# Wide products that nobody reads, put between the router's steps on TensorE

## The reference, cut to what matters

```
def ec_moe(h, w_router, w_gate, w_up, w_down):
    xt = h.reshape(n, D)
    aff = jax.nn.softmax((xt @ w_router).astype(jnp.float32), axis=-1)
    cap = CAPACITY_FACTOR * n // N_EXPERTS
    gate, idx = lax.top_k(aff.T, cap)
    xe = jnp.take(xt, idx, axis=0)
    hid = jax.nn.silu(jnp.einsum('ecd,edf->ecf', xe, w_gate)) * jnp.einsum('ecd,edf->ecf', xe, w_up)
    ye = jnp.einsum('ecf,efd->ecd', hid, w_down) * gate[..., None].astype(h.dtype)
    out = jnp.zeros_like(xt).at[idx.reshape(-1)].add(ye.reshape(-1, D))
```

## Time and profile before

| what | value |
|---|---|
| time, median of 3 runs | 1823.35 us |
| the profiled execution's own time | 1822.89 us |
| its span, first to last instruction | 1821.1 us |
| TensorE (PE) busy | 1668.2 us, 92% of the span |
| VectorE, ScalarE busy | 510.3 us, 298.2 us |
| moved by DMA | 638.52 MB, mean 351 GB/s |
| mean granted TensorE clock | 0.984 of full speed |

### The profile page before, as it was taken

The page is one execution under the profiler, slowest core; times in us unless marked ns, Lnnn a source line. Parts: engine busy times, 40 slices in busy tenths (PEclk is TensorE's granted clock), DMA queues, the critical chain, the costliest instruction groups (busy, mean ns, idle before and its releaser), DMA issues.

```text
span 1821.1 us, 19170 instructions
## 1 busy us (share of the span) xinstructions
PE 1668.2 (92%) x7900; PEld 792.5 (44%) x7900; DVE 510.3 (28%) x982; ACT 298.2 (16%) x635; POOL 47.8 (3%) x72
## 2 busy tenths in 40 slices
PE   6999999999999999888898888889888998889897
PEld 3767777778884333332232232323222233223232
DVE  4575647775670201111010111101011111101103
ACT  2453354563330000000000000000000000000001
POOL 2010000011000000000000000000000000000001
PEclk9999999999979999999999999999999999999999
DMA  9873232226587999999999999999999999999996
GB/s 346 285 281 105 71 128 92 93 93 215 221 362 317 425 395 432 427 434 429 431 429 431 429 432 431 428 431 431 430 432 429 432 430 430 431 428 431 431 430 269
DMA packets 65023, 638.52 MB, mean 351 GB/s; under 512 B 5653, under 2 KB 5837, under 8 KB 36557
## 3 DMA queue, kind: packets, MB, share of 16 engines
q1 hardware_dynamic: 61648, 629.83, 83.0%
q0 software_dynamic: 3328, 8.04, 1.4%
HBM read 634.14 MB, written 3.70 MB: 350 GB/s over the span
## 4 chain that ended last, share of the span: by engine, by line
DMA 50%; PE 47%; DVE 3%; issue 0%; ACT 0%; SPq 0%; ACTq 0%; DVEq 0%
DMA ring<-in_w_exp_gate 23%; DMA ring<-in_w_exp_up 23%; PE banks L877 17%; PE banks L1296 15%; DMA ring<-in_w_exp_down 4%; PE banks L1415 2%; PE banks L875 2%; PE banks L829 1%; PE banks L1278 1%; PE banks L892 1%; PE banks L1078 1%; PE banks L1233 1%; PE banks L873 1%; PE banks L1035 1%; PE banks L1009 1%; DMA ring<-in_w_mod 1%
## 5 line engine op out<-in xcount | busy, mean ns | idle before, releaser
L1296 PE MATMUL banks<-ring,O 128*64 128x512 f32 x3048 | 657.0, 582 | 81.7 <-DMA ring<-in_w_exp_up 60.5
L1296 PEld LDWEIGHTS banks<-ring,O 128*64 128x64 f32 x3048 | 211.9, 135 | 528.0 <-issue 421.9
L1415 PE MATMUL banks<-ring,O 128*64 128x512 f32 x1400 | 317.7, 609 | 37.7 <-DMA ring<-in_w_exp_down 33.2
L1415 PEld LDWEIGHTS banks<-ring,O 128*64 128x64 f32 x1400 | 98.9, 140 | 245.4 <-issue 183.8
L877 PE MATMUL banks<-slot_parts,X_parts 128*128 128x512 f32 x672 | 184.3, 403 | 0.0
L2240 DVE TENSOR_TENSOR O<-O,banks 128x512 f32<-128x512 f32 (+1 forms) x48 | 30.9, 644 | 515.7 <-PE banks L1296 487.3
L1724 ACT ACTIVATE O<-banks 128x512 f32<-128x512 f32 (+1 forms) x48 | 23.7, 563 | 736.3 <-PE banks L1296 736.3
L877 PEld LDWEIGHTS banks<-slot_parts,X_parts 128*128 128x128 f32 x672 | 121.2, 188 | 39.4 <-issue 11.8
L2220 DVE TENSOR_TENSOR X<-X,banks 128x512 f32<-128x512 f32 x90 | 61.9, 688 | 190.6 <-PE banks L1278 190.6
L1850 DVE TENSOR_TENSOR slot_parts<-ring,slot_parts 128x512 fp32r<-128x512 f32 x168 | 105.7, 688 | 16.6 <-ACT slot_parts L1471 15.9
L2253 DVE TENSOR_TENSOR O<-banks,O 128x512 f32<-128x512 f32 x32 | 20.7, 686 | 319.4 <-PE banks L1415 319.4
(11 more groups left out here) (296 smaller groups left out, 1136.2 us busy)
## 6 DMA issues: line engine op xcount, KB each, us to landing
ring<-in_w_exp_up SPq DMA_DIRECT2D x61, 2816.0 KB, 33.8
ring<-in_w_exp_gate SPq DMA_DIRECT2D x58, 2816.0 KB, 32.1
ring<-in_w_exp_down SPq DMA_DIRECT2D x29, 3072.0 KB, 28.3
ring<-in_w_exp_down SPq DMA_DIRECT2D x14, 4096.0 KB, 31.6
ring<-in_w_in SPq DMA_DIRECT2D x16, 2048.0 KB, 8.8
ring<-in_w_exp_down SPq DMA_DIRECT2D x24, 1024.0 KB, 33.2
ring<-in_w_mod SPq DMA_DIRECT2D x16, 512.0 KB, 11.4
O<-in_w_mod SPq DMA_DIRECT2D x8, 1024.0 KB, 5.2
```

Source lines behind the costliest of these rows:

```text
L1296: x = pe.matmul(banks[64 * w:64 * w + 64, 3 * m + b, 0:(i1 - i0) * P], xeT[:, 2 * (k % 4) + k // 4, :], w4[:, w, i0 * P:i1 * P], start=(k ...
L1415: x = pe.matmul(banks[64 * w:64 * w + 64, (4 if last else 6) + dc, :], hidT[:, i, 64 * w:64 * w + 64], rows[:, w, dc * BANK:(dc + 1) * BAN ...
```

## The change

35 products are added to TensorE's list, in 12 places (one of them in a loop that runs four times) between the end of the mixer and the first expert's products. Each multiplies 64 columns of the identity with 512 columns of `ring` (the start of quarter 5, the first expert's second up quarter) into partitions 0 to 63 of bank 7 or bank 0. Nobody reads what they write. A wait for that quarter's transfer (`land_u[1]`) is added ahead of them, and a second `wait_job_copied(pe, J_WO[-1])` before the first of them that writes bank 0. Nothing is removed, and the order of all other instructions is as it was.

```diff
+            def keep_clock(n, bank=0):
+                for i in range(n):
+                    pe.matmul(banks[0:64, bank, :], ident[:, 0:64], reg(5 * QUARTER, BANK), start=True, stop=True)
+            pe.wait_ge(land_u[1], 16)
             pe.wait_ge(h2_norm, 1)
             turn_tile(h2, 0)
+            keep_clock(2, 7)
             shift_logits()
+            keep_clock(1, 7)
             pe.wait_ge(h2_norm, 2)
             turn_tile(h2, 1)
+            keep_clock(2, 7)
             pe.wait_ge(shift_row, 1)
             for n in range(2):
                 for b in range(2):
                     logits(n, b)
+                    keep_clock(2, 7)
+            wait_job_copied(pe, J_WO[-1])
             pe.wait_ge(h2_half_done, 1)
             turn_half(h2, 2, 0)
+            keep_clock(1)
             turn_probs(0)
             turn_probs(1)
+            keep_clock(1)
             pe.wait_ge(h2_half_done, 2)
             turn_half(h2, 2, 1)
-            for b in range(2):
-                logits(2, b)
+            keep_clock(2)
+            logits(2, 0)
+            keep_clock(2)
+            logits(2, 1)
+            keep_clock(8)
             wait_job_copied(pe, J_WO[-1])
...
             turn_probs(2)
             pe.wait_ge(rt_part, 1)
             pe.matmul(banks[:, 1, 0:CAP_L], one_expert(0), slots[:, 0:CAP_L], start=True, stop=True).then_inc(rt_first, 1)
+            keep_clock(2)
...
             pe.wait_ge(sel_ready, 2)
             first_gather((2, 3, 6, 7), (1, 2))
+            keep_clock(4)
             pe.wait_ge(rt_part, 2)
             pe.matmul(banks[:, 1, CAP_L:SLOT], one_expert(0), slots[:, CAP_L:SLOT], start=True, stop=True).then_inc(rt_first, 1)
             first_gather((4, 5), (1, 2))
             pe.wait_ge(sel_ready, 3)
             first_gather((2, 3, 6, 7), (0,)).then_inc(xet_done, 1)
             first_gather((0, 1), (1, 2))
+            keep_clock(2)
```

## The result

The changed kernel takes 1849.34 us, the median of 4 runs (1848.85 to 1850.16), against 1823.51 us before: ratio 1.0142, 95% interval 1.0127 to 1.0157, so 25.8 us slower. The forecast was 1846.6 us, in a range of 1841 to 1860.

What follows compares the result with a forecast made beforehand. The path to the first expert products bounds the kernel: 20.84 us of old work plus 31.5 of new replace 29.09, 23.3 later; 1822.89 + 23.3 = 1846.2, median 0.46 higher, forecast 1846.6 us, range 1841 to 1860.

Steps and rivals of the forecast that it cites:

- What bounds the kernel: Way to the first expert products: one microsecond there is one of the whole; the experts behind have no slack.
- The price of one product: Added products, mixer's end to first experts: 0.90 us each at full clock, 35 cost 31.5 us.
- The other work at full clock: TensorE's old router work: turns 2.91, shift 0.50, logits 6.60, probability turns 0.45, two further products 0.63 us together.
- rival B: The clock doesn't hold in the router: 1867 us, or 1880 if it never returns before the experts; chance 0.18.
- The gathers: 40 records before the first expert product: 0.244 us each at either clock, so 9.75 us stay.
- The clock at the first expert products: Clock falls after about 6 us of late narrow gather work; the same 2 us are lost as before the change.
- A: Forecast case: clock holds, products 0.9 us each, 1846.6; own range 1842 to 1851, chance 0.77; low: prices -0.9, clock held -2.0.
- The waits: Router: first tile's logits 531.9, selection start 541.1, slots 549.9 us; 5.6 of the eight products' 7.2 us hold up selection.
- Rival C: Not slower: products stream once, 0.228 us each, 8.0 against 8.3 us given back; about 1823.1; chance 0.05 including slack in experts.
- its point of decision: Product price below which the change is not slower: 0.24 us, or 0.29 where the clock also holds to the experts.

Runs made afterwards that it cites:

- the run in the experts: Kernel before plus two unread wide float products after each expert's second combination group from the second expert on, 30 in all: 1825.37 us, ratio 1.0010.
- contiguous runs: First expert's gather takes 128 neighbouring columns of h2 instead of every eighth: 1841.12 us on the changed kernel, 1821.31 us on the kernel before.
- the no-eight run: Changed kernel without the eight wide products behind the last logits: 1846.78 us, ratio 1.0129.
- the one-pass run: Changed kernel with its 35 products on 16-bit floats, so that each streams its 512 columns once: 1831.28 us, ratio 1.0051.

## Why the prediction was right, point by point

- *What bounds the kernel* was right: the table above shows the end moving with the transfer behind the first expert products, one for one. Only "the experts run as fast as their weights arrive" was an average: the run in the experts shows that TensorE still sets the pace until 650 us, where one more product costs its full time as well.
- *The price of one product* was right: 0.90 said, 0.876 in the run of eight and 0.93 in pairs. A single one among narrow work takes 1.00. Eleven groups of them made the router a little longer than the sum: the slot product came at 556.8 and not at 555.7, the differences being seams, where wide and narrow work meet (a tile's logits cut in two take 2.3 us, not 2.20).
- *The other work at full clock* was right: the clock held (rival B fell), each half of a tile's logits took 1.0 us. That it would hold was a judgment and not a working: no row of before has wide products among such narrow work. The versions with less wide work show how near it was: the clock fell by 530 with one-pass products, at 542.5 with one float product a place, and near 527 with seven in all.
- *The gathers* gained nothing from the clock, as the one row of the last eight records had shown: 0.246 us at 1.00. The rule that the prediction takes from the Trainium skill, "TensorE: Matmul & The Clock Gate", on warm and cold products would have misled here, by 4.9 us. The contiguous runs show the reason, which the prediction didn't give: the stride. Without it the rule nearly holds, 0.119 against 0.222.
- *The clock at the first expert products* was the mis-sized term. I let the clock fall once, in the 24 records of the late gathers, and priced the four products before them at full clock, 3.6 us. It fell already at the end of the first 16 records, and the four took 6.45: +2.85 us. It then rose, and fell again where I had it. With the 1.1 us of seams that is nearly all of the 4.0 us by which the first expert product was later than forecast. The range held it (I had +2 to +4 for it), the forecast didn't. By its own terms, though, the low end of A is 1846.6 - 0.9 - 2.0 = 1843.7 and not 1842. The loss varies, as the no-eight run with 5.14 us shows, which may be why the median is 1.4 us kinder than the profiled run.
- *The waits* were right one by one: 532.3 for the first tile's maximum (531.9 said), 542.05 for the first MAX8 (541.1), slots at 551.3 (549.9), 5.3 of the eight's 7 us exposed (5.6).
- *Rival C*, not slower, fell on its price, and the one-pass run shows that its point of decision, 0.24 to 0.29 us, was too kind, because it takes for granted that the clock holds: at 0.28 us a product the kernel is still 8 us slower, with its clock at 0.50 in three stretches between 530 and 560.

## What to carry to other kernels

Before buying a clock with dummy work, add up what the engine does on the path at the full clock, and set the saving against the price: here 8.3 us against 31. Work that nobody reads is free only where something else ends the wait, and in a stretch that is short of TensorE such places are few; 30 such products among the experts cost 0.08 us each instead of 0.74, and nearly all of that falls on the first two, which stand where TensorE still sets the pace. A mean over a long stretch doesn't show such a place. Look first at why a narrow product is slow: a strided stationary operand doubled its time at the full clock (at the low one it added a tenth), and storing the columns in the order of their use was worth more than any placing of the wide products that was tried.

## What the runs showed of the hardware

- The granted clock fell to 1.2 GHz with TensorE busy 33 of 33 us, when that was weight loads, transposes and products of 16 or 32 columns; with 512-column products between them, one to eight at a place, it stayed at 2.4 GHz for 40 us. With one at a place it stayed there for 21 us and then fell. The busy column of a profile does not tell the clock.
- A float product with 128 stationary columns at a step of 32 bytes takes 0.246 us a record at 2.4 and at 1.2 GHz; contiguous, 0.119 and 0.222.
- Reads at a step of 32 bytes, written out contiguously, slow ScalarE's 1024-column pass from 1.25 to 2.33 us, and VectorE's 512-column passes from 1.00 to 1.40 us for two.
